# Second norm and output row of each token moved from a closing phase into the later of its two expert pairs

## What is computed

```python
def _hier_moe(x, w_group, b_group, w_expert, b_expert, w_gate_up, w_down):
    ...
    g_sel = jnp.argmax(g_logits + b_group.astype(jnp.float32), axis=-1)
    ...
    _, top_i = lax.top_k(e_sel + e_bias, TOP_K)
    ...
    expert_idx = g_sel[:, None] * EXPERTS_PER_GROUP + top_i
    ...
    for e in range(N_EXPERTS):
        gu = xt @ w_gate_up[e]
        h = jax.nn.silu(gu[:, :D_EXPERT]) * gu[:, D_EXPERT:]
        y = y + gate[:, e:e + 1] * (h @ w_down[e]).astype(jnp.float32)
    ...
    ffn = _hier_moe(x1, w_group, b_group, w_expert, b_expert, w_gate_up, w_down)
    return _layernorm(ALPHA * x1 + ffn, ln2_g, ln2_b)
```

## Time and profile before

| what | us |
|---|---|
| median of 3 runs | 649.16 (648.3 to 650.5) |
| the profiled execution | 649.52 |
| its span in the profile | 647.3 |
| PE busy | 546.3 (84%) |
| DVE busy | 288.9 (45%) |
| ACT busy | 138.2 (21%) |
| POOL busy | 124.4 (19%) |

### The profile page before, as it was taken

One profiled execution on the slowest core, in us unless ns is written; L12 is line 12 of the kernel. 1 busy time (PEld: TensorE's weight loads), 2 busy tenths in 40 slices (PEclk: granted clock), 3 DMA queues, 4 the chain that ended last, 5 costly groups with the idle time before them and its releaser, 6 DMA issues.

```text
span 647.3 us, 8402 instructions
## 1 busy us (share of the span) xinstructions
PE 546.3 (84%) x3194; PEld 289.7 (45%) x3194; DVE 288.9 (45%) x657; ACT 138.2 (21%) x263; POOL 124.4 (19%) x163
## 2 busy tenths in 40 slices
PE   6999999999799878999981899997878888788390
PEld 5887888863255433455541233332322223232130
DVE  1721048498735666532564332342441123021776
ACT  1000192222335531231310011201010101010221
POOL 1001053500128610000001213111121112111033
PEclk9999999999899999999985799997988889798795
DMA  9930007610609341009777199999999999993343
GB/s 307 408 101 5 0 17 311 235 62 1 262 13 406 167 147 38 2 33 404 291 304 306 50 413 420 418 422 425 423 425 421 422 419 421 424 414 136 126 172 123
DMA packets 26335, 160.13 MB, mean 247 GB/s; under 512 B 8120, under 2 KB 8152, under 8 KB 16512
## 3 DMA queue, kind: packets, MB, share of 16 engines
q1 hardware_dynamic: 17680, 131.98, 50.4%
q0 software_dynamic: 7008, 27.43, 10.9%
q10 hardware_dynamic: 1616, 0.30, 0.3%
HBM read 155.66 MB, written 13.34 MB: 261 GB/s over the span
## 4 chain that ended last, share of the span: by engine, by line
PE 64%; DMA 21%; DVE 9%; ACT 3%; issue 2%; SPq 1%; POOLq 0%; DVEq 0%; ACTq 0%
PE ps L469 21%; DMA arena_w<-in_w_gu 18%; PE ps L905 13%; PE ps L707 8%; PE ps L922 3%; PE ps L610 2%; PE ps L548 2%; PE ps L594 2%; DVE arena_s L1359 2%; PE ps L631 1%; PE ps L770 1%; PE ps L895 1%; PE ps L514 1%; DVE bn L1488 1%; DMA arena_s<-x_rows,gidx 1%
## 5 line engine op out<-in xcount | busy, mean ns | idle before, releaser
L905 PE MATMUL ps<-arena_w,arena_s 128*64 128x512 f32 x368 | 122.0, 673 | 27.3 <-DMA arena_o<-in_w_gu 14.2
L469 PE MATMUL ps<-arena_w 128*128 128x260 f32 (+1 forms) x448 | 100.6, 387 | 6.2 <-DMA arena_w<-in_w_in 6.2
L469 PEld LDWEIGHTS ps<-arena_w 128*128 128x128 f32 (+1 forms) x448 | 84.4, 189 | 21.9 <-DMA arena_w<-in_w_in 6.2
L905 PEld LDWEIGHTS ps<-arena_w,arena_s 128*64 128x64 f32 x368 | 36.5, 155 | 109.1 <-issue 91.6
L1729 DVE TENSOR_TENSOR arena_s<-arena_s,ps 128x256 f32<-128x256 f32 x16 | 6.7, 421 | 138.6 <-ACT arena_s L1186 138.6
L707 PE MATMUL ps<-arena_o,arena_s 128*128 128x512 f32 x128 | 60.0, 615 | 1.6 <-DVE arena_s L1483 1.6
L922 PE MATMUL ps<-arena_w,cs 128*64 128x512 f32 x184 | 54.8, 598 | 6.9 <-ACT cs L1188 6.9
L905 PE MATMUL ps<-arena_o,arena_s 128*64 128x512 f32 x112 | 55.2, 651 | 0.0
L1961 POOL DMA_INDIRECT arena_s<-x_rows,gidx x18 | 19.5, 1083 | 168.6 <-DVE gidx L1689 115.3
L1707 DVE TENSOR_SCALAR arena_s<-ps,vec 128x128 f32<-128x128 f32 x136 | 44.9, 403 | 11.1 <-PE ps L895 11.1
L1359 DVE STREAM_TRANSPOSE arena_s<-arena_w 128x1024 f32<-128x1024 f32 x36 | 41.8, 1214 | 8.6 <-PE ps L548 8.5
(11 more groups left out here) (316 smaller groups left out, 695.5 us busy)
## 6 DMA issues: line engine op xcount, KB each, us to landing
arena_w<-in_w_gu SPq DMA_DIRECT2D x23, 2048.0 KB, 15.9
arena_w<-in_w_dn SPq DMA_DIRECT2D x23, 1024.0 KB, 17.2
arena_o<-in_w_gu SPq DMA_DIRECT2D x7, 2048.0 KB, 22.5
arena_o<-in_w_dn SPq DMA_DIRECT2D x7, 1024.0 KB, 22.0
arena_w<-in_w_in SPq DMA_DIRECT2D x13, 512.0 KB, 14.9
arena_o<-in_w_out SPq DMA_DIRECT2D x1, 4096.0 KB, 13.8
arena_s<-in_w_gu SPq DMA_DIRECT2D x2, 2048.0 KB, 10.2
arena_w<-pair_rows SPq DMA_DIRECT2D x8, 512.0 KB, 6.7
```

What stands on the lines that cost most here:

```text
L469: last = mm(ps[rows, b + n, 0:HALF], lhs(k), rhs(k)[:, n * HALF:(n + 1) * HALF], start=(k == 0), stop=(k == ks - 1))
L905: last = mm(ps[64 * e:64 * e + 64, 2 + q, :], xgT[:, k, CAP * e:CAP * (e + 1)], gu_w[2 * slots + e][:, k, :], start=(k == 0), stop=(k == K ...
```

## The change

**Pairing.** The weights are laid out so that pair k holds experts k and k+16. The two experts of a token lie in one group of 8, so they are now always in different pairs: its first pair and its later pair.

**What a pair does now.** All tokens of a pair add their own expert's row, times its gate, to the residual, which DVE makes from the gathered `x1` rows themselves (`residual`, `own_part`). The plain expert rows of tokens whose first pair this is are scattered to `first_rows` (`scatter_own`); for tokens whose later pair it is, the row of the first pair is gathered from `first_rows` (`gather_other`), added, normalised (`finish`) and scattered straight to `y_out` (`scatter_out`). Indices outside the tensor are skipped, which is how one tile serves both kinds. The gates and the indices of each (token, choice) are a row of 8 numbers in `info_rows`, gathered once per pair (`gather_info`).

**What moves.** The gates are computed before the first pair, between DVE's first copy of tokens and the marking of the second slot table, and are sent to `info_rows` by 7 DMAs on ACT's queue. The copy of turned tokens is shared: four of its eight pieces go to ACT (`tokens_out` on ACT). ACT copies the whole 1024 columns of the down product; DVE no longer copies any. Gathered rows have 4 buffers (before 2), the gather of pair n+3 stands in the turn of pair n, behind a wait for `out_landed`, the landing of the `scatter_out` of pair n-1, whose buffer it reuses. Gains and biases of the norms are loaded before the loop. `first_rows` is filled once from `x_tok` at about 114 us, so that no row is undefined. The closing phase is gone.

The core of the diff:

```diff
+            landed(sp, x1_stored, TT)
+            sp.dma_start(lng, lns[0:2].partition_broadcast(P)).then_inc(ln1_landed, 16)
+            sp.dma_start(lng2, lns[2:4].partition_broadcast(P)).then_inc(ln2_landed, 16)
...
-            sp.wait_ge(dn_ps, 3)
-            sp.dma_start(lng, lns[0:2].partition_broadcast(P)).then_inc(ln1_landed, 16)
-            sp.dma_start(lng2, lns[2:4].partition_broadcast(P)).then_inc(ln2_landed, 16)
...
-            for q in range(NPAIR):
-                sp.wait_ge(scattered[q], n_rounds * (NGRP * 16))
...
-                sp.dma_start(y1[t][0:n, :], pair_rows[P * t:P * t + n, :]).then_inc(y_landed[t], 16)
-                sp.dma_start(y2[t][0:n, :], pair_rows[HALF_ID + P * t:HALF_ID + P * t + n, :]).then_inc(y_landed[t], 16)
...
-                sp.dma_start(y_out[P * t:P * t + ROWS[t], :], y1[t][0:ROWS[t], :]).then_inc(y_stored, 16)
...
+                if not last_pair:
+                    turn_tokens(it, n + 1)
+                pe.wait_ge(h_ready, nth(it, n, add=1))
```

ACT's part, new:

```diff
+            def tokens_out(it, n):
+                act.wait_ge(xt_ps, nth(it, n, add=1))
+                if n > 0:
+                    act.wait_ge(gu_ps, nth(it, n))
+                for k in range(KD // 2, KD):
+                    last = fn(xgT[:, k, :], ps[:, k // 4, (k % 4) * P:(k % 4 + 1) * P], ACT.Identity,
+                              bias=vec[:, V_LB + k:V_LB + k + 1], scale=vec[:, V_LG + k:V_LG + k + 1])
+                last.then_inc(xt_act, 1)
...
+            def hidden(it, n, last_pair=False):
+                act.wait_ge(gu_ps, nth(it, n, add=1))
+                fn(sg, ps[:, 2 + n % 2, 0:DE], ACT.Silu).then_inc(silu_done, 1)
+                if not last_pair:
+                    tokens_out(it, n + 1)
+                act.wait_ge(ht_ps, nth(it, n, add=1))
+                nc.scalar.copy(hT, ps[:, 4, 0:2 * P].rearrange("p (f n) -> p f n", f=2)).then_inc(ht_sb, 1)
+
+            def own_out(it, n):
+                act.wait_ge(dn_ps, nth(it, n, add=1))
+                if n >= 2:
+                    act.wait_ge(scattered, nth(it, n - 1, 1, 16))
+                    act.wait_ge(own_added, nth(it, n - 1))
+                nc.scalar.copy(yb[n % 2].rearrange("p (a b) -> p a b", a=2), ps[:, 5:7, :]).then_inc(ya_done, 1)
+
+            def root(it, n):
+                act.wait_ge(mean_done, nth(it, n, add=1))
+                fn(stat[:, 2:3], stat[:, 1:2], ACT.Sqrt, bias=eps[:, 1:2]).then_inc(root_done, 1)
...
+            with act.Fori(0, n_rounds * 4 - 1) as it:
+                for j in range(4):
+                    hidden(it, FIRST + j)
+                    own_out(it, FIRST + j)
+                    root(it, FIRST + j - 1)
...
+            hidden(last, FIRST, True)
+            root(last, FIRST - 1)
+            root(last, FIRST)
```

DVE's part (the gates' lines, 1754 to 1775 of before, now stand right behind `tokens_out(None, 0)`; the index arithmetic behind them is cut):

```diff
+            def tokens_out(it, n):
+                dve.wait_ge(xt_ps, nth(it, n, add=1))
+                if n > 0:
+                    dve.wait_ge(gu_ps, nth(it, n))
+                for k in range(KD // 2):
                     last = ts(xgT[:, k, :], ps[:, k // 4, (k % 4) * P:(k % 4 + 1) * P], vec[:, V_LG + k:V_LG + k + 1],
                               vec[:, V_LB + k:V_LB + k + 1], ALU.mult, ALU.add)
...
+            def hidden(it, n):
+                dve.wait_ge(silu_done, nth(it, n, add=1))
+                tt(hx, sg, ps[:, 2 + n % 2, DE:2 * DE], ALU.mult).then_inc(h_ready, 1)
...
+            def residual(it, n):
+
+                x = xg[n % 4]
+                stt(x, x, ALPHA, lng[:, 0, :], ALU.mult, ALU.mult).then_inc(res_scaled, 1)
+                dve.wait_ge(res_scaled, nth(it, n, add=1))
+                stt(x, lng[:, 1, :], ALPHA, x, ALU.mult, ALU.add).then_inc(res_ready, 1)
...
+            def own_part(it, n, last_pair=False):
+
+                x, gate = xg[n % 4], info[:, n % 4, 0:1]
+                dve.wait_ge(info_landed[n % 2], nth(it, n, 2, 16, 16))
+                dve.wait_ge(res_ready, nth(it, n, add=1))
+                if last_pair:
+                    dve.wait_ge(dn_ps, nth(it, n, add=1))
+                    y = ps[:, 5:7, :]
+                    x = x.rearrange("p (a b) -> p a b", a=2)
+                else:
+                    dve.wait_ge(ya_done, nth(it, n, add=1))
+                    y = yb[n % 2]
+                stt(x, y, gate, x, ALU.mult, ALU.add).then_inc(own_added, 1)
...
+            def finish(it, n):
+
+                x = xg[n % 4]
+                dve.wait_ge(own_added, nth(it, n, add=1))
+                if n > 0:
+                    dve.wait_ge(yo_landed[n % 2], nth(it, n + 1, 2, 16))
+                    stt(x, yo[n % 2], info[:, n % 4, 1:2], x, ALU.mult, ALU.add).then_inc(other_added, 1)
...
+                V.bn_stats(bn[:, 0, :], x[:, 0:512])
+                V.bn_stats(bn[:, 1, :], x[:, 512:D]).then_inc(bn_done, 1)
...
+                V.memset(stat[:, 2:3], 0.0)
+                V.bn_aggr(stat[:, 0:2], bn[:, :, :]).then_inc(mean_done, 1)
+                dve.wait_ge(mean_done, nth(it, n, add=1))
+                stt(x, x, stat[:, 0:1], lng2[:, 0, :], ALU.subtract, ALU.mult).then_inc(centred, 1)
+                dve.wait_ge(root_done, nth(it, n, add=1))
+                V.reciprocal(stat[:, 2:3], stat[:, 2:3]).then_inc(rstd_done, 1)
+                dve.wait_ge(rstd_done, nth(it, n, add=1))
+                dve.wait_ge(centred, nth(it, n, add=1))
+                stt(x, x, stat[:, 2:3], lng2[:, 1, :], ALU.mult, ALU.add).then_inc(out_ready, 1)
...
+                own_part(None, n)
+                residual(None, n + 1)
+            with dve.Fori(0, n_rounds * 4 - 1) as it:
+                for j in range(4):
+                    n = FIRST + j
+                    hidden(it, n)
+                    tokens_out(it, n + 1)
+                    finish(it, n - 1)
+                    own_part(it, n)
+                    residual(it, n + 1)
+            last = n_rounds, dve.value_load(rounds[0:1, 1:2], min_val=NE // 2 - 2, max_val=MAXR * NE // 2)
```

POOL's part, new (each register value is set ahead of its wait):

```diff
+            def gather_rows(it, n):
...
+                if n >= 4:
+                    pool.wait_ge(out_landed[n % 2], out)
+                if n >= 4 and n % 2 == 0:
+                    pool.wait_ge(raw_landed, table)
+                    for b in range(2):
+                        pool.wait_ge(info_landed[b], infos)
+                    load_slots(it, n + 2)
+                b, r = gidx[:, n % 4:n % 4 + 1], raw[:, n // 2 % 2, n % 2:n % 2 + 1]
+                G.tensor_scalar(b, r, HALF_ID, -HALF_ID, ALU.is_ge, ALU.mult).then_inc(idx_half, 1)
+                fixed()
+                pool.wait_ge(idx_half, half)
+                G.tensor_tensor(b, b, r, ALU.add).then_inc(idx_half, 1)
+                fixed()
+                pool.wait_ge(idx_half, both)
+                G.indirect_dma_start(out=xg[n % 4], out_offset=None, in_=x1_rows,
+                                     in_offset=bass.IndirectOffsetOnAxis(ap=gidx[:, n % 4:n % 4 + 1], axis=0),
+                                     bounds_check=TOK - 1, oob_is_err=False).then_inc(gathered[n % 4], 16)
...
+            def gather_info(n):
+                G.indirect_dma_start(out=info[:, n % 4, :], out_offset=None, in_=info_rows,
...
+            def scatter_own(it, n):
...
+                pool.wait_ge(ya_done, copied)
+                G.indirect_dma_start(out=first_rows, out_offset=bass.IndirectOffsetOnAxis(ap=info_i[:, n % 4, 2:3], axis=0),
+                                     in_=yb[n % 2], in_offset=None, bounds_check=TOK - 1,
+                                     oob_is_err=False).then_inc(scattered, 16)
...
+            def gather_other(it, n):
...
+                pool.wait_ge(scattered, there)
+                G.indirect_dma_start(out=yo[n % 2], out_offset=None, in_=first_rows,
...
+            def scatter_out(it, n):
...
+                pool.wait_ge(out_ready, ready)
+                G.indirect_dma_start(out=y_out, out_offset=bass.IndirectOffsetOnAxis(ap=info_i[:, n % 4, 3:4], axis=0),
+                                     in_=xg[n % 4], in_offset=None, bounds_check=TOK - 1,
+                                     oob_is_err=False).then_inc(out_landed[n % 2], 16)
...
+            with pool.Fori(0, n_rounds * 4 - 1) as it:
+                for j in range(4):
+                    n = FIRST + j
+                    scatter_own(it, n)
+                    scatter_out(it, n - 1)
+                    gather_other(it, n + 1)
+                    gather_rows(it, n + 3)
+                    gather_info(n + 3)
...
+            scatter_out(last, FIRST - 1)
+            scatter_out(last, FIRST)
```

438 lines of the change are left out of this document (187 added, 251 removed).

## The result

The changed kernel takes 687.58 us, median of 4 runs (684.06 to 698.84), against 648.73 us (646.95 to 650.50) for the kernel before. The ratio is 1.059, 95% interval 1.054 to 1.065: slower, as forecast, but by 39 us instead of 13, and 1.6 us above the top of the range.

A forecast was written before the change was run, and what follows sets the result against it. The prediction took the weight stream to bound the expert loop, with PE bounding the first pairs. Its terms, -32.2 + 7.3 + 1.6 + 36.2 = +12.9 on the profiled 649.5 us, gave 662 us; range 630 to 686.

The forecast's parts named there:

- Term 1: After the last down product: the closing phase shrinks from 43.6 to 11.4 us, -32.2 us.
- Term 3: ACT in a pair: four token pieces ahead of its hidden-row copy cost 0.8 us for pairs 0 and 1, +1.6 us.
- Term 2: Start, before the first pair: gates ahead of the slot marks (+4.8) and gain loads ahead of the first gather (+2.5), +7.3 us.
- Term 4: Expert loop, POOL's turn: one full landing in series makes a turn L + 6.7 us, a pair every 18.4 us; +36.2 us.
- L: Landing time of a row DMA beside the weight stream in POOL's turn, taken as 11.7 us; one microsecond worth 13.
- The formula: Loop from D(1) to D(15), the down products of pairs 1 and 15: added time is 13 L - 115.9 us.
- rival (b): POOL's turn in the loop: L lies between, 9.5 to 10.7 us, giving 637 to 649 us; chance 0.14.
- (a): Expert loop: rows keep up and weights set the pace, needing L at or below some 9.5; 630 us, chance 0.20.
- (c): POOL's queue itself is full, 4 us for each DMA, a turn of 22 us; 702 us, chance 0.08.
- (d): End of kernel: the closing phase stays for tokens in some case, such as a second round of experts; given no chance.

The follow-up runs named there:

- tuned kernel: Changed kernel with 4 KB weight packets, landings taken out of POOL's turn, and start and end mended (also called the mended kernel): 636.93 us, ratio 0.984 to the kernel before.

## Why the prediction was right in direction and wrong in size

**What bounds the kernel.** Right. After the change PE waits for `x_rows`, POOL for landings of `out_y` and `first_rows`, and the rate is below 400, all as the last part of the prediction had it.

**Term 1, the closing phase: -32.2, measured -23.3.** This step failed, at the 0.5 us that the sum had as an estimate for the end of the program. From D(15) to the issue of the last scatter are 8.5 us, where the sum had 7.6, and the landing took 3.3, as forecast. Then 8.4 us followed instead of 0.5, 8.1 of them POOL's drain. The trace of before holds that drain of 7.4 us, but I had not looked at what follows an engine's last instruction, since the chain of waits ended on SP. The change makes POOL the engine that ends last, and so exposes it.

**Terms 2 and 3, the start and ACT: +8.9, measured +8.7.** Right in sum. The gather behind the gain loads cost 3.1 us (2.5 forecast, bounds 0 and 5.4), and the first product starts 7.8 us later (7.3). Of the 1.6 us of Term 3 only 0.9 came: a pair that PE bounds takes 13.4 instead of 12.4 us (0.8 forecast), but the first pair is no longer than before, since its gate and up product took 8.66 us instead of 9.76. The tuned kernel shows that all of Term 2 could be avoided by order alone.

**Term 4, POOL's turn: +36.2, measured +49.4.** The mechanism was right: landings in series in POOL's turn, which the experiments remove in two ways. The term failed in size, and not by L. The fixed part of a turn, put at 6.7 us, is 8.8, while the landing of finished rows averaged 11.1 us, a little under the 11.7 forecast. Of the 2.1 us more, 1.3 are POOL's waits for DVE's finished rows and ACT's copy (9.2 and 5.1 us in the eleven turns), which the sum had put at nothing, and 0.7 is the way from the first index operation to the gather, 2.1 us instead of 1.4. The whole, piece by piece against the forecast: eleven turns of 19.9 instead of 18.4 us, +16.8; the first landing 10.8, -0.9; from it to the tokens of pair 4 3.8 instead of 3.3, +0.5; the last gather 6.3 instead of 11.7, as the weight stream ran out beside it (1.6 MB of it from 634.5 to 641 us), -5.4; from there to D(15) 21.0 instead of 18.8, +2.2. That is +13.2, and 36.2 + 13.2 = 49.4.

The formula seems to fit when the median of `out_y`, 12.7, is put in: 13 x 12.7 - 115.9 = 49.2. That is chance. What eleven turns add up is the mean, and with 11.1 the formula gives 28.4. Nor does any run show by itself that a microsecond of L is worth 13: with shorter landings the weights soon set the pace.

**The range.** By the prediction's own sum L from 10.8 to 13.2 gives 650 to 682 us, not 652 to 685, and L = 9.5 gives 633, not the 637 of rival (b). The 8.9 us of Term 1 stood outside every case; with them the top, 686, would have reached 695. The 22.0 us by which the profiled execution missed the forecast are 8.9 of Term 1, 13.2 of Term 4 and -0.2 of Terms 2 and 3.

**The rivals.** (a) did not come, but the small packets show that its condition was real: with landings of 7 us instead of 12 the weights set the pace again. They gave 646 us and not 630, since the end took 8.9 us more than Term 1 had and D(1) to D(15) 227.0 instead of 220.3. The mended kernel comes to 636. (b) asked for an L of 9.5 to 10.7, and the mean was 11.1. (c) is the rival whose time, 702, lies nearest to the result, but with the wrong cause: its queue would have been full in the run without weights as well. (d) did not come: no closing phase is left in the profile.

The estimate of 2.6 us for such a DMA, from the Trainium skill (DMA: Bandwidth & Descriptors, "Anatomy of one DMA — SWDGE (gpsimd) path"), is near the medians of the row DMAs in the run with hardly any weights, 2.6 to 4.3 us, and far below those beside the stream, 6.7 to 12.7.

**Where the gain went.** The closing phase did shrink by 23 us. It was spent twice over in POOL's turns, which hold a landing beside the weight stream, 4 to 17 us long and 11 in the mean, and 8.8 us of POOL's own work and waits.

## What to carry to other kernels

Before a small DMA is put in series with anything in a loop, take its landing time from the loop's own stretch, at the place in the queue that it will have, and multiply by the number of turns. Take the mean and not the median when times add up over turns, and list what else the engine waits for in a turn. Follow each buffer around the ring, for a landing that is taken out of one engine's order comes back through the buffer's next writer. Look at the packets of the big stream beside a small DMA: cutting these from 16 and 8 to 4 KB was worth 41 us here, and cost 11 where no landing was on the path. And look at what an engine does after its last instruction before making it the last one to finish.
